# Picking sorted token rows with 0/1 matrices on TensorE instead of a scatter and loads

## What is computed

```python
he = jax.nn.silu(hf @ w1[e]) * (hf @ w3[e])
y = y + combine[:, e:e + 1] * (he @ w2[e])
```

## Time and profile before

| What | Value |
|---|---|
| Median of 3 runs | 1927.25 us (1923.77 to 1929.41) |
| The profiled execution: its time | 1927.59 us |
| The profiled execution: its span | 1925.8 us, mean granted clock 0.93 |
| PE busy | 1755.5 us (91%) |
| DVE busy | 726.9 us (38%) |
| ACT busy | 246.6 us (13%) |
| POOL busy | 114.0 us (6%) |
| Mean DMA rate | 174 GB/s over the span |
| Chain that ended last | PE 83%, DVE 9%, DMA 3% |

### The profile page before, as it was taken

One profiled execution on the slowest core, in us unless ns is written; L12 is line 12 of the kernel. 1 busy time (PEld: TensorE's weight loads), 2 busy tenths in 40 slices (PEclk: granted clock), 3 DMA queues, 4 the chain that ended last, 5 costly groups with the idle time before them and its releaser, 6 DMA issues.

```text
span 1925.8 us, 16687 instructions
## 1 busy us (share of the span) xinstructions
PE 1755.5 (91%) x6670; PEld 957.9 (50%) x6670; DVE 726.9 (38%) x1288; ACT 246.6 (13%) x531; POOL 114.0 (6%) x121
## 2 busy tenths in 40 slices
PE   6999969998999999999889899997996584999997
PEld 1444458744555444444656588543754553333332
DVE  0383352244777600103246466003157834111112
ACT  1100041201000100000125111000111121111110
POOL 0000000000000000000100000002022201000001
PEclk9999965599999999999999899998998676999999
DMA  9445310002746532221630389534432116999997
GB/s 348 148 146 204 117 62 22 1 22 90 259 160 233 185 121 87 87 72 59 232 113 1 109 311 358 204 133 118 168 139 82 60 44 220 394 389 388 393 389 279
DMA packets 160684, 334.46 MB, mean 174 GB/s; under 512 B 15192, under 2 KB 15472, under 8 KB 160608
## 3 DMA queue, kind: packets, MB, share of 16 engines
q1 hardware_dynamic: 141408, 298.87, 42.9%
q0 software_dynamic: 18288, 31.37, 5.0%
q10 hardware_dynamic: 912, 3.17, 0.4%
HBM read 355.58 MB, written 15.48 MB: 193 GB/s over the span
## 4 chain that ended last, share of the span: by engine, by line
PE 83%; DVE 9%; DMA 3%; issue 2%; ACT 2%; POOL 1%; SPq 0%; DVEq 0%; POOLq 0%; ACTq 0%
PE psum L559 79%; PE psum L563 4%; DMA wring<-in_w_mod 1%; POOL small L1286 1%; ACT wide L1417 1%; DMA y_slots<-lnb 1%; DVE big L1960 0%; DVE small L1814 0%; ACT big L1417 0%; DVE xres L1821 0%; DVE big L2125 0%; DVE big L2144 0%; DMA wide<-y_slots,slot_i 0%; DVE small L2143 0%; DVE wide L2195 0%
## 5 line engine op out<-in xcount | busy, mean ns | idle before, releaser
L559 PE MATMUL psum<-wring,big 128*128 128x512 f32 (+1 forms) x1536 | 559.9, 598 | 12.9 <-issue 9.5
L559 PE MATMUL psum<-wide,wring 128*128 128x256 f32 (+3 forms) x1648 | 512.6, 476 | 3.4 <-DVE wide L1785 3.4
L559 PEld LDWEIGHTS psum<-wring,big 128*128 128x128 f32 (+1 forms) x1536 | 231.7, 173 | 326.1 <-issue 325.3
L559 PEld LDWEIGHTS psum<-wide,wring 128*128 128x128 f32 (+2 forms) x1648 | 268.5, 181 | 137.5 <-issue 112.8
L1747 DVE SCALAR_TENSOR_TENSOR wide<-wring,csilu,wide 128x512 f32<-128x512 f32 x364 | 250.3, 747 | 3.0
L559 PE MATMUL psum<-wring,wide 128*128 128x512 f32 (+2 forms) x512 | 208.2, 554 | 0.0
L1799 DVE TENSOR_TENSOR wide<-psum,gate 128x512 f32<-128x512 f32 x28 | 19.3, 691 | 361.7 <-PE psum L559 361.5
L559 PE MATMUL psum<-big,wide 128*64 128x512 f32 (+2 forms) x568 | 137.0, 544 | 3.9 <-DVE wide L1883 3.9
L559 PEld LDWEIGHTS psum<-const,wide 128*128 128x128 f32 x480 | 88.7, 199 | 94.9 <-issue 85.1
L1417 ACT ACTIVATE big<-psum 128x512 f32<-128x512 f32 (+1 forms) x153 | 79.9, 534 | 429.1 <-PE psum L559 398.6
L559 PEld LDWEIGHTS psum<-wring,wide 128*128 128x128 f32 x512 | 90.9, 190 | 77.6 <-issue 75.9
(11 more groups left out here) (252 smaller groups left out, 1003.7 us busy)
## 6 DMA issues: line engine op xcount, KB each, us to landing
wring<-in_mlp_w SPq DMA_DIRECT2D x32, 2048.0 KB, 8.7
wring<-in_w SPq DMA_DIRECT2D x32, 2048.0 KB, 20.8
wring<-in_w_mod SPq DMA_DIRECT2D x24, 2048.0 KB, 10.4
big<-in_w SPq DMA_DIRECT2D x23, 2048.0 KB, 20.5
wide<-in_w SPq DMA_DIRECT2D x14, 2048.0 KB
wring<-in_w_ada SPq DMA_DIRECT2D x12, 2048.0 KB, 9.2
wring<-in_w_in SPq DMA_DIRECT2D x8, 2048.0 KB, 8.5
wring<-in_ev_w_in SPq DMA_DIRECT2D x6, 2048.0 KB, 13.6
```

Source lines behind the costliest of these rows:

```text
L559: return nc.tensor.matmul(o, a, b, start=first, stop=last)
```

## The change

The slots' rows are no longer written to DRAM and loaded again. The normalised rows stay in SBUF as `xn2`. For each group DVE writes a matrix `member_of` (256 tokens by 128 slots, double-buffered) with a one where the token sits in the slot; a slot without a token has a column of zeros. PE multiplies the rows with it, which picks and transposes at once: 16 matmuls in place of 8 transposes. The scatter, the loads, the blank write to `x_slots` and the semaphores `x_spread` and `xs_in` go. `yT2` moves to make room for `xn2`, `slot_f` moves, and a constant `count` (0 to 127 in each row) is added to the constants that are loaded at the start.

```diff
-                  ("late", LATE * SLOTS)])
+                  ("late", LATE * SLOTS), ("count", P)])
...
+    put("count", t)
...
-        yT2 = region(big, 0, KC, T)
+        yT2 = region(big, 2048, KC, T)
...
-        slot_f = region(lnb_flat, 1248, 2, 2)
+        slot_f = region(small, 536, 2, 2)
...
-        xs = region(big, 0, 2, D)
+        xn2 = region(big, 0, 2, D)
+
+        at_f, at_p = CONST_COLS["cum_f"][0], CONST_COLS["perm"][0]
+        member_of = (region(const, at_f, 2, P), region(const, at_p, 2, P))
+        slot_rel = region(small, 540, 2, 2, 2)
...
-            turn_x("moe", xn, (0, 1))
+            turn_x("moe", xn2, (0, 1))
...
             def turn_group(g):
                 n = GROUP_AT[g]
-                pe.wait_ge(xs_in[n % 2], 16 * (n // 2 + 1))
+                pe.wait_ge(members_ready, n + 1)
                 if n > 0:
                     pe.wait_ge(hs_ready, 2 * n)
                 for k in range(KC):
-                    last = turn(psum[:, 4 + k // 4, (k % 4) * P:(k % 4 + 1) * P], xs[:, n % 2, k * P:(k + 1) * P])
+                    for t in range(2):
+                        last = mm(psum[:, 4 + k // 4, (k % 4) * P:(k % 4 + 1) * P], xn2[:, t, k * P:(k + 1) * P],
+                                  member_of[n % 2][:, t, :], t == 0, t == 1)
                 last.then_inc(xs_turned, 1)
...
                 if n == 0:
                     sp.wait_ge(table_ready, 1)
-                    sp.wait_ge(x_spread, 64)
...
-            pool.dma_start(x_slots.rearrange("(g p) n -> p g n", p=P),
-                           tmp[:, 0:D].unsqueeze(1).to_broadcast([P, GROUPS, D])).then_inc(blank_out, 16)
...
-            pool.wait_ge(blank_out, 32)
-            pool.wait_ge(slots_ready, 1)
-            for c in range(2):
-                for t in range(2):
-                    at = slot_i[:, 2 * c + t:2 * c + t + 1]
-                    pool.indirect_dma_start(out=x_slots, out_offset=bass.IndirectOffsetOnAxis(ap=at, axis=0),
-                                            in_=xn[:, t, :], in_offset=None).then_inc(x_spread, 16)
-            pool.wait_ge(x_spread, 64)
-
-            def load_group(n):
-                g = GROUP_ORDER[n]
-                if n > 1:
-                    pool.wait_ge(xs_turned, n - 1)
-                pool.dma_start(xs[:, n % 2, :], x_slots[g * P:(g + 1) * P, :]).then_inc(xs_in[n % 2], 16)
-
-            begins = sorted(BEGINS)
-            loaded = 0
+            pool.wait_ge(blank_out, 16)
             for i in range(UNITS - LATE):
-                while loaded < GROUPS and (loaded < 2 or begins[loaded - 2] <= i + 1):
-                    load_group(loaded)
-                    loaded += 1
...
-            assert loaded == GROUPS
+            pool.wait_ge(slots_ready, 1)
...
             signal(v_.tensor_copy(slot_i[:, :], slot_f.rearrange("p c t -> p (c t)")), slots_ready)
+
+            def members(n):
+
+                if n > 1:
+                    dve.wait_ge(xs_turned, n - 1)
+                rel, of = slot_rel[:, n % 2], member_of[n % 2]
+                step(v_.tensor_scalar(rel, slot_f, float(P * GROUP_ORDER[n]), None, ALU.subtract))
+                for t in range(2):
+                    last = v_.tensor_scalar(of[:, t, :], cst("count"), rel[:, 0, t:t + 1], None, ALU.is_equal)
+                step(last)
+                for t in range(2):
+                    last = v_.scalar_tensor_tensor(of[:, t, :], cst("count"), rel[:, 1, t:t + 1], of[:, t, :],
+                                                   ALU.is_equal, ALU.add)
+                signal(last, members_ready)
+
+            members(0)
...
+            members(1)
             modulate_group(0)
...
                 if i + 1 in BEGINS:
                     modulate_group(BEGINS[i + 1])
+                    if GROUP_AT[BEGINS[i + 1]] + 1 < GROUPS:
+                        members(GROUP_AT[BEGINS[i + 1]] + 1)
                 if i > 0:
                     keep_y(i - 1)
```

More of the change, by code:

```diff
@@ L399, in build @@
         rel_scratch = nc.dram_tensor("rel_scratch", [8, 2 * T - 1], F32, kind="Internal").ap()
-        x_slots = nc.dram_tensor("x_slots", [GROUPS * P, D], F32, kind="Internal").ap()
         y_slots = nc.dram_tensor("y_slots", [UNITS * SLOTS, D], F32, kind="Internal").ap()
@@ L477, in build @@
         blank_out = sem("blank_out")
-        x_spread = sem("x_spread")
-        xs_in = [sem(f"xs_in{a}") for a in range(2)]
+        members_ready = sem("members_ready")
         xs_turned = sem("xs_turned")
@@ L1831, in head_rate, with rms_row @@
                 root(v_.tensor_scalar(out_rate, out_rate, 1.0 / width, eps, ALU.mult, ALU.add), out_rate)
-            def rms_row(t):
+            def rms_row(t, xn):
                 x = xres[:, X0 + t, :]
@@ L1854, in mlp @@
                     if l == 1:
-                        rms_row(t - X0)
+                        rms_row(t - X0, xn)
             mods(0, 0, 4)
@@ L2261, in _ @@
                     residual(2, "out2", half, (X0 + t,), alpha=1.0)
-                rms_row(t)
+                rms_row(t, xn2)
             modulate("moe")
```

## The result

The changed kernel takes 1942.97 us, the median of four runs (1941.39 to 1945.93). The kernel before takes 1927.72 beside it. The ratio is 1.0084, with a 95% interval of 1.0063 to 1.0105: slower by 15.3 us. The profiled execution took 1941.69 us (span 1939.9), 14.1 more than the one before.

The account below looks back on a forecast made before the run. PE was taken to set the pace, with a slightly slow weight stream adding stalls. Start 0, groups +29.5, stalls -7.8, constants +0.2, end -0.7 gave +21.2 us: 1948.5 us, range 1941 to 1957.

Parts of the forecast that it names:

- Rival (4): Expert stage goes by bytes and PE takes the new records into slack: faster, ending near 1915 us; chance 0.04.
- The eleven groups: Expert stage after group 0: 32 PE records per group take 3.70 us instead of 1.02, +29.5 us in all.
- Rival (3): PE's records cost less than 0.112 us each, weight loads hidden better: 1934 to 1941 us; chance 0.07.
- The stream: Weight loads in the expert stage: without the sorted rows the stream has slack and PE's stalls go, -7.8 us.
- Rival (1): PE's stalls stay, because they come from the order of landings, not lack of bandwidth: 1956 us; chance 0.12.
- The start: From the known slots through group 0 and the first units: taken as 0, bounds -0.9 and +3.6 us.
- better case: At the start, the clock rises 5 us after PE's work begins, so unit 0 loses nothing: -0.9 us.
- second case: At the start, the clock rises some 9.5 us after group 0's start; unit 0 loses 0.4: +1.1 us.
- Rival (2): The start costs its upper bound, the clock staying low through group 0 and 6 us of unit 0: 1952; chance 0.08.
- DVE: Making the `members` matrices and waiting for them in the expert stage is hidden behind PE's work: cost 0.
- Rival (5): DVE becomes late and puts 1.5 us per group on the path: 1965 us; chance 0.02.
- Elsewhere and the end: Blank write gone, worth 0; extra constants at kernel start, +0.2 us; earlier gathers before the last adds, -0.7 us.

Follow-up runs that it names:

- e1: Changed kernel with 8 transposes per group in place of the 16 matmuls, still without the sorted rows' loads (it picks nothing): 1911.93 us, ratio 0.9917.
- m1c: As m1, but the sorted rows of groups 9, 10 and 11 are loaded by SP only if the table needs them: 1918.76 us, ratio 0.9951.
- a0: The changed kernel run once more without any edit: 1945.09 us, ratio 1.0088.
- e3: Changed kernel, but DVE makes matrices for the first two groups only and the others reuse them: 1944.16 us, ratio 1.0082.
- m1: Changed kernel, but only group 0 picked by matrices; scatter and loads return for the other eleven: 1924.55 us, run again 1924.1 us.
- m3: As m1, but groups 0, 8 and 1 are picked by matrices, the other nine by scatter and loads: 1925.73 us, ratio 0.9989.
- b2: Changed kernel with rows split into two bf16 parts and bf16 matrices, 32 one-record matmuls per group: 1925.41 us, ratio 0.998.
- b1: As b2, but only the rounded bf16 part is kept, 16 one-record matmuls per group: 1913.06 us, ratio 0.9923.
- e2: Kernel before, with its scatter and loads, but each group turned by 16 two-record matmuls in place of 8 transposes: 1946.98 us, ratio 1.0094.

## Why the prediction was right, step by step

- **What bounds.** Right. PE sets the pace, and the stream was in deficit. e1, with full DMA engines and no stall, shows that a DMA share of 1.05 alone does not bind this stage. Rival (4), faster by the bytes, fell: it would have needed PE to take its records into slack, and PE took none.
- **The eleven groups.** Predicted 3.70 each and +29.5, measured 3.92 and +30.2. The difference per group was 2.68 and is 2.75. The new groups and the old ones were both priced 0.2 low, because I took 10.97 for a unit and 1.02 for a group where the steps between the `he` turns give 10.82 and 1.17. Rival (3), cheaper records, fell: the pitch is (3.84-0.275)/31 = 0.115. By the Trainium skill's figure, 81 ns in "TensorE: Matmul & The Clock Gate", section "Back-to-back issue gap", the groups would have cost +18.6, an estimate from the page. The rows disagree with it in both types, 0.115 in fp32 and 0.055 in bf16.
- **The stream.** Right in kind: all stalls went. Its size was off: -10.0, not -7.8, since I summed the marked idle time. That is the largest mis-sized term of the stage. Rival (1), that all stalls stay, fell with the result. Its cause, the order of landings, is not needed either: m1c's 3.6 us for 1.5 MB are what bandwidth gives, though no run changed the order alone. The DMA share did not fall to 0.9 but to 0.98, while the rate fell to 353 GB/s, 0.905 of 390; here the share said less than the rate.
- **The start.** Taken as 0 with a bound of -0.9. Against the one profile of the kernel before it is -2.2 twice (the changed kernel and a0) and -0.4 to -0.8 in five more that pick group 0 with the same 32 records (e3, m1 twice, m3, m1c). What differs is the time at which the granted clock rises from 0.50 to 1.00: 2.7 us after PE's turn of the picks began in the first two, 5.1 to 6.1 us after it in the other five. The prediction's better case had 5 us, read from 32 transposes of 6.36 us as some 22 records at the half rate; redone, the sum gives 25 and 5.5 us, and the granted clock rises there at about 928.5, 5.5 us after 923.07. So -0.9 was a fair value of the usual case, 0 was a little high, and the rest of the -2.2 is luck of the profiled execution. The second case, a rise "as late as now" (9.5 us after the group began), came in none of the seven; b2 and b1, with shorter groups, had 9.1 and 9.5 us from the picks' turn. Of the -2.2, the faster unit 0 gives 2.9, and the later first matmul takes back 0.7 (unit 0 begins 17.4 us after the slots instead of 16.7). Rival (2), the full price of a late clock, did not come in any of the runs.
- **DVE.** Right, 0 (e3). `members` took 1.33, predicted 1.5. Rival (5) fell.
- **Elsewhere and the end.** The blank write is worth nothing in its window, and the +0.2 of the constants is too small to be seen. The end gave 0.8, predicted 0.7: the gathers end before the last `keep_y`. That the emptier stream made them early, as the prediction had it, is not shown. The last store of `y_slots` still took 9 us to land, and every other kernel here ends in 18.1 us too, also m1, whose stream is full and makes PE wait as late as 1882.8.
- **The sum.** 30.2 - 10.0 - 2.2 - 0.8 = +17.2 from the slots on. The medians of the changed kernel give +15.3 and, as a0, +17.1 against the kernel before on their chips; part of this spread is the chance ahead of the slots. The prediction's +21.2 was 4 us too high: 2.2 from the stalls and 2.2 from the start, the latter partly luck, while the groups were 0.7 too low.

Where did the gain of the idea go? The bytes that were saved are worth the 10 us of stalls that PE's new records would have removed anyway (e2). Most of the scatter path hid behind the late picks, and the 32 records of group 0 take back more than half of what its removal gave in the start (e1: 4.9 us; with the records: 2.2). e1 shows what the removal alone is worth: 17 us. PE's picking costs 32, and the sum is the loss.

## What to carry to other kernels

When two resources are full at once, find the one that the other waits for: work added to it is paid in full, and it refunds the stalls only once, whichever edit removes them. Before a gather is moved to TensorE, count its records: an fp32 matmul of two contraction tiles is four records where a transpose is one. And price the type: in bf16 the same picking costs half per record (b2), and with one rounded part no more than the transposes (b1). Picking the first group alone gained 3.5 us after the slots (m1), only 0.7 of it in the start for which it was meant, and a conditional load was worth as much again (m1c).

## What the runs showed of the hardware

- A bf16 record of 128 columns with its own 128x128 weights follows the next at 0.055 us at full clock, the fp32 one at 0.112 to 0.115, and a fp32 matmul is two of them.
- The 32 fp32 records of group 0 took 4.60, 4.60, 6.22, 5.76, 5.91, 6.07 and 6.16 us in seven profiles (the changed kernel, a0, e3, m1, m1 again, m3, m1c). PE's instructions ahead of them are the same in all seven. The granted clock rose 2.7 us after PE's turn of the picks began in the first two and 5.1 to 6.1 us after it in the others.
- The same instructions brought the routing to its end at 1616.2 and at 1619.0 in two profiles of one kernel. A difference of 3 us ahead of an edit is no effect of the edit.
